# A fused decoder layer: second halves of the up weights at another SBUF place, key scores by query block, no zero matmuls

## The reference, cut to what matters

```python
def peer(x, w_query, sub_keys_1, sub_keys_2, expert_down, expert_up):
    q = (x @ w_query).reshape(B, S, PEER_HEADS, 2, PEER_QDIM // 2)
    s1 = jnp.einsum('bshc,kc->bshk', q[..., 0, :], sub_keys_1)
    s2 = jnp.einsum('bshc,kc->bshk', q[..., 1, :], sub_keys_2)
    ...
    # top 16 of each half -> 256 candidates -> top 16, softmax: gates and expert_idx
    u = expert_down[et]
    h = jax.nn.gelu(jnp.einsum('cd,ced->ce', xt, u), approximate=False)
    vv = expert_up[et]
    return jnp.einsum('ce,ced->cd', gt * h, vv)
```

## Time and profile before

| | |
|---|---|
| median of 3 runs | 2463.01 us (2461.73 to 2466.8) |
| the profiled execution | 2464.3 us |
| its span, first to last instruction | 2462.6 us |
| mean granted TensorE clock | 0.997 |
| TensorE matmuls busy | 2432.2 us, 99% of the span |
| VectorE, ScalarE, GpSimd busy | 60%, 47%, 23% |
| chain that ended last | PE 98% (L1119 66%, L1324 28%) |

### The profile page before, as it was taken

The page is one execution under the profiler, slowest core; times in us unless marked ns, Lnnn a source line. Parts: engine busy times, 40 slices in busy tenths (PEclk is TensorE's granted clock), DMA queues, the critical chain, the costliest instruction groups (busy, mean ns, idle before and its releaser), DMA issues.

```text
span 2462.6 us, 49767 instructions
## 1 busy us (share of the span) xinstructions
PE 2432.2 (99%) x17939; PEld 2292.9 (93%) x17940; DVE 1487.3 (60%) x2444; ACT 1166.8 (47%) x1660; POOL 556.0 (23%) x379
## 2 busy tenths in 40 slices
PE   8999999999999999999999999999999999999997
PEld 8999999999999999999999999999888888888886
DVE  5555554546666667688888644444555555555556
ACT  5444444554544445655555544444444444444444
POOL 0000000000000000468888888800000000000000
PEclk9999999999999999999999999999999999999999
DMA  7767766554445655578888888876766777667764
GB/s 266 223 216 229 225 215 197 190 186 153 153 154 171 196 194 177 170 214 214 208 226 214 218 218 213 222 254 214 234 231 234 240 243 239 226 238 241 241 231 140
DMA packets 179845, 521.15 MB, mean 212 GB/s; under 512 B 52768, under 2 KB 52768, under 8 KB 179536
## 3 DMA queue, kind: packets, MB, share of 16 engines
q1 hardware_dynamic: 124128, 449.89, 56.0%
q0 software_dynamic: 51056, 53.83, 10.1%
q10 hardware_dynamic: 4608, 16.78, 1.7%
HBM read 484.64 MB, written 35.78 MB: 211 GB/s over the span
## 4 chain that ended last, share of the span: by engine, by line
PE 98%; DVE 1%; issue 0%; ACT 0%; DMA 0%; ACTq 0%; DVEq 0%; SPq 0%
PE ps L1119 66%; PE ps L1324 28%; PE ps L1158 1%; PE ps L1173 1%; PE ps L1166 0%; PE ps L1160 0%; PE ps L1293 0%; PE ps L1174 0%; PE ps L1153 0%; DVE u_s L1072 0%; DMA raw<-stream 0%; DVE u_s L1082 0%; DVE y_s L1059 0%; DVE w_first L670 0%; ACTq L603 0%
## 5 line engine op out<-in xcount | busy, mean ns | idle before, releaser
L670 DVE TENSOR_TENSOR w_first<-raw,w_first 128x1024 fp32r<-128x1024 f32 x425 | 520.7, 1225 | 568.0 <-ACT w_first L382 548.5
L1119 PE MATMUL ps<-a_hi,w_first 128*128 128x256 f32 x3728 | 684.2, 279 | 12.3 <-DVE w_first L670 12.3
L1119 PE MATMUL ps<-a_hi,w_second 128*128 128x256 f32 x3728 | 672.6, 276 | 0.0
L670 DVE TENSOR_TENSOR w_second<-raw,w_second 128x1024 fp32r<-128x1024 f32 x425 | 520.0, 1223 | 165.3 <-ACT w_second L382 165.2
L1119 PEld LDWEIGHTS ps<-a_hi,w_first 128*128 128x128 f32 x3728 | 581.0, 188 | 13.2 <-issue 9.1
L1119 PEld LDWEIGHTS ps<-a_hi,w_second 128*128 128x128 f32 x3728 | 578.6, 188 | 0.0
L382 ACT ACTIVATE w_second<-raw 128x1024 fp32r<-128x1024 f32 x425 | 448.0, 1054 | 186.9 <-PE ps L1324 183.7
L1119 PE MATMUL ps<-a_lo,w_first 128*128 128x256 f32 x1864 | 516.3, 277 | 0.0
L1119 PE MATMUL ps<-a_lo,w_second 128*128 128x256 f32 x1864 | 514.6, 276 | 0.0
L353 POOL DMA_INDIRECT g_dram<-gate_v,where x256 | 459.4, 1795 | 114.7 <-issue 80.4
L382 ACT ACTIVATE w_first<-raw 128x1024 fp32r<-128x1024 f32 x425 | 447.8, 1054 | 30.9 <-issue 14.1
(11 more groups left out here) (205 smaller groups left out, 2483.6 us busy)
## 6 DMA issues: line engine op xcount, KB each, us to landing
raw<-stream SPq DMA_DIRECT2D x850, 512.0 KB
g_dram<-blank POOLq DMA_DIRECT2D x32, 512.0 KB, 6.2
a_dram<-act ACTq DMA_DIRECT2D x32, 512.0 KB
a_in<-a_dram POOLq DMA_DIRECT2D x32, 512.0 KB, 5.1
g_in<-g_dram POOLq DMA_DIRECT2D x32, 512.0 KB, 6.3
g_dram<-gate_v,where POOLq DMA_INDIRECT x256
res<-x_t SPq DMA_DIRECT2D x4, 512.0 KB, 6.7
ln_s<-ln POOLq DMA_DIRECT2D x1, 2048.0 KB, 7.5
```

Of the source, the lines that this page charges most:

```text
L670: dve.tensor_tensor(w_lo[s][:, :], raw[:, s, :], w_hi[s][:, :].bitcast(F32), ALU.subtract).then_inc(lo_ready, 1)
L1119: ins = pe.matmul(out, w, a, start=first and q == 0, stop=last and q == 2)
```

## The change

The second halves of the up weights, from up tile 2 on, are split into `up_hi` and `up_lo`. These are views into `a_hi` and `a_lo`, 16 elements (64 bytes) behind their start, at 128 modulo 512. The tiles 0 and 1 keep `w_second`, since their halves are split while the down stage still reads `a_hi` and `a_lo`. The first round of 8 up tiles is written out ahead of the loop on ScalarE, VectorE and TensorE. The zero matmuls, `zero`, and VectorE's memset with its wait are gone; the first up tile starts its banks with `start=True`. Score groups and transposes alternate the token block (`g % 2`) and go through the query blocks in order (`g // 2`); each waits for the blocks that it reads. A wait for `h1_lo` stands ahead of the down loop.

```diff
-    zero = sb("zero", [P, 512], mybir.dt.bfloat16, up_mem)
+    up_hi = a_hi.rearrange("p k t -> p (k t)")[:, 16:16 + 2 * HALF].rearrange("p (s n) -> p s n", s=2)
+    up_lo = a_lo.rearrange("p k t -> p (k t)")[:, 16:16 + 2 * HALF].rearrange("p (s n) -> p s n", s=2)
+
+    def weights(t, hf, moved=False):
+
+        return (up_hi[:, t.par, :], up_lo[:, t.par, :]) if moved and hf else (w_hi[t.slot(hf)], w_lo[t.slot(hf)])
...
-                act.activation(w_hi[t.slot(hf)][:, :], raw[:, t.slot(hf), :], ACT.Copy).then_inc(hi_ready, 1)
+                act.activation(weights(t, hf, moved)[0], raw[:, t.slot(hf), :], ACT.Copy).then_inc(hi_ready, 1)
...
-            act.activation(sc[:, g // 4, 4 * (g % 4):4 * (g % 4) + 4, :], spare[g % 4].rearrange("p (a n) -> p a n", a=4),
+            act.activation(sc[:, g % 2, 4 * (g // 2):4 * (g // 2) + 4, :], spare[g % 4].rearrange("p (a n) -> p a n", a=4),
...
-            act.activation(h1_n[:, g // 4, 512 * (g % 4):512 * (g % 4) + 512], spare[g % 4], ACT.Copy).then_inc(ht_ready, 1)
+            act.activation(h1_n[:, g % 2, 512 * (g // 2):512 * (g // 2) + 512], spare[g % 4], ACT.Copy).then_inc(ht_ready, 1)
...
-                hi(t.next())
+                hi(t.next(), moved=not first or b > 0)
...
-        with act.Fori(0, NKEYS // 8 - 1) as i:
+        up_tiles(0, False, True)
+        with act.Fori(1, NKEYS // 8 - 1) as i:
...
-                dve.tensor_tensor(w_lo[s][:, :], raw[:, s, :], w_hi[s][:, :].bitcast(F32), ALU.subtract).then_inc(lo_ready, 1)
+                high, low = weights(t, hf, moved)
+                dve.tensor_tensor(low, raw[:, s, :], high.bitcast(F32), ALU.subtract).then_inc(lo_ready, 1)
...
-        dve.wait_ge(ag_in[0], 32)
-        dve.memset(zero[:], 0.0).then_inc(z_ready, 1)
...
-        pe.wait_ge(q_done, KD)
         pe.wait_ge(keys_in, 16)
         for g in range(8):
-            tt, c0 = g // 4, 4 * (g % 4)
+            tt, c0 = g % 2, 4 * (g // 2)
+            pe.wait_ge(q_done, c0 + 4)
...
         for g in range(8):
-            tt, c0 = g // 4, 4 * (g % 4)
+            tt, c0 = g % 2, 4 * (g // 2)
             pe.wait_ge(sc_ready, g + 5) if g < 4 else pe.wait_ge(ht_ready, g - 3)
-            pe.wait_ge(h1_ready, KD)
+            pe.wait_ge(h1_ready, c0 + 4)
...
+        pe.wait_ge(h1_lo, KD)
...
-        pe.wait_ge(z_ready, 1)
...
-        for c in range(8):
-            pe.matmul(ps[:, 512 * c:512 * c + 512], zero[:, 0:P], zero[:], start=True, stop=False, skip_group_check=True)
-
-        def up(t, n, b):
+
+        def up(t, n, b, moved=True, first=False):
...
+                high, low = weights(t, hf, moved)
                 for tt in range(TT):
                     s = slice(P * tt, P * tt + P)
-                    for m, w in ((m_hi, w_hi), (m_hi, w_lo), (m_lo, w_hi)):
+                    for q, (m, w) in enumerate(((m_hi, high), (m_hi, low), (m_lo, high))):
                         for c in range(2):
                             o = D * tt + HALF * hf + 512 * c
-                            ins = pe.matmul(ps[:, o:o + 512], m[:, b % 2, s], w[t.slot(hf)][:, 512 * c:512 * c + 512],
-                                            start=False, stop=False, skip_group_check=True)
+                            ins = pe.matmul(ps[:, o:o + 512], m[:, b % 2, s], w[:, 512 * c:512 * c + 512],
+                                            start=first and q == 0, stop=False, skip_group_check=True)
...
-        with pe.Fori(0, NKEYS // 8 - 1) as i:
+        for b in range(8):
+            up(Tile(T_UP + b), b, b, b > 1, b == 0)
+        with pe.Fori(1, NKEYS // 8 - 1) as i:
```

More of the change, by code:

```diff
@@ L252, in build @@
     m_ready, mhi_ready, mlo_ready, y_ready = sem("m_ready"), sem("mhi_ready"), sem("mlo_ready"), sem("y_ready")
-    z_ready, nmean_ready, sd_ready, out_ready, y_done = (
-        sem("z_ready"), sem("nmean_ready"), sem("sd_ready"), sem("out_ready"), sem("y_done"))
+    nmean_ready, sd_ready, out_ready, y_done = (
+        sem("nmean_ready"), sem("sd_ready"), sem("out_ready"), sem("y_done"))
     dve_step, act_step = sem("dve_step"), sem("act_step")
+    up_hi = a_hi.rearrange("p k t -> p (k t)")[:, 16:16 + 2 * HALF].rearrange("p (s n) -> p s n", s=2)
+    up_lo = a_lo.rearrange("p k t -> p (k t)")[:, 16:16 + 2 * HALF].rearrange("p (s n) -> p s n", s=2)
+    def weights(t, hf, moved=False):
+        return (up_hi[:, t.par, :], up_lo[:, t.par, :]) if moved and hf else (w_hi[t.slot(hf)], w_lo[t.slot(hf)])
     r_sq = h1_n.rearrange("p t (q n) -> p (t q) n", q=2)
@@ L375, in _, with hi @@
             act.sem_inc(a_out[b], 16)
-        def hi(t, halves=(0, 1)):
+        def hi(t, halves=(0, 1), moved=False):
             for hf in halves:
@@ L628, in _, with up_tiles @@
             gelu(t, b, NKEYS // 8 - 1)
-        def up_tiles(i, last):
+        def up_tiles(i, last, first=False):
             for b in range(8):
@@ L663, in _, with lo @@
         dve.sem_inc(m_ready, 8)
-        def lo(t, halves=(0, 1)):
+        def lo(t, halves=(0, 1), moved=False):
             for hf in halves:
@@ L1041, in up_tiles @@
                     break
-                lo(t.next())
+                lo(t.next(), moved=not first or b > 0)
                 n = i * 8 + b if not last else NKEYS - 8 + b
@@ L1048, in up_tiles @@
                 m_low(n + 1, (b + 1) % 2)
-        with dve.Fori(0, NKEYS // 8 - 1) as i:
+        up_tiles(0, False, True)
+        with dve.Fori(1, NKEYS // 8 - 1) as i:
             up_tiles(i, False)
@@ L1332, in up_bank @@
             w = slice(512 * (c % 2), 512 * (c % 2) + 512)
[L1333 to L1336, removed]
-        with pe.Fori(0, NKEYS // 8 - 1) as i:
+            high, low = weights(t, c // 2, True)
+            pe.matmul(ps[:, o:o + 512], m_hi[:, b % 2, s], high[:, w], start=False, stop=False, skip_group_check=True)
+            pe.matmul(ps[:, o:o + 512], m_hi[:, b % 2, s], low[:, w], start=False, stop=False, skip_group_check=True)
+            return pe.matmul(ps[:, o:o + 512], m_lo[:, b % 2, s], high[:, w], start=False, stop=False, skip_group_check=True)
+        for b in range(8):
+            up(Tile(T_UP + b), b, b, b > 1, b == 0)
+        with pe.Fori(1, NKEYS // 8 - 1) as i:
             for b in range(8):
```

## The result

The changed kernel takes **2451.14 us** (2450.02 to 2451.9, 6 runs), and the one before 2463.2 us (2461.73 to 2466.8, 6 runs) beside it: ratio 0.9946, with a 95% interval of 0.9935 to 0.9956. That is 0.54% less. The prediction said 2451.9 us. The profiled execution takes 2450.02 us, and its span is 2448.3 us.

A forecast was written before the change was run, and what follows sets the result against it. TensorE's own stream was taken to bound the kernel: 4.2 + 1.4 + 5.5 = 11.1 us off the profiled 2464.3 gives 2453.2, and with the runs' median 1.3 us lower, 2451.9 us; 8-in-10 range 2449.5 to 2457.8.

The forecast's parts named there:

- Key scores: At the scores behind the query projection: waiting by group removes TensorE's idle time and the low clock, 4.2 us less.
- All three parts: At the key scores: 2.45 us of idle time, 1.65 us of low clock and 0.1 us in the first group.
- the scores don't gain: Rival at the key scores: first copy late or clock falls anyway, the wait only moves; 2456.1 us, 8% chance.
- Zero matmuls: Between down and up stage: without the zeros the first up matmul starts earlier, 1.4 us less, ends 1.3 and 1.5.
- hand-over: At the first up rows: 0.2 us of the starts put down to the change from the zeros, some of it remaining.
- Moved halves: In the up stage: second halves at 128 modulo 512 save 0.044 us a tile over 126 tiles, 5.5 us less.
- The settled pace: In the up stage: 229 against 233 ns per matmul, giving the moved halves' upper end of 6.0 us.
- the place modulo 512: In the up stage: the moving operand's place, 128 against 256, makes matmuls take 229 instead of 233 ns.
- The rule that spoke against it: Skill's "PE and ACT never wait on anyone": by it the up stage's moved halves bring 0, the sum 5.6 us.
- A slower rhythm: Rival in the up stage: new halves settle 8 ns slower per matmul, 24.2 us more, 2476.1 us; 6% chance.

The follow-up runs named there:

- experiment 8: Kernel before with `w_second` itself at 128 modulo 512 in every stage, no new home: 2466.64 us, from 2458.42 to 2488.84 in 12 runs, ratio 1.0022.
- Experiment 3: Changed kernel with the moved halves 48 instead of 16 elements into `a_hi` and `a_lo`, at 256 modulo 512: 2457.46 us, ratio 0.997.
- experiment 4: Changed kernel with the second halves at eight places 64 bytes apart, by the tile's position in a round: 2454.91 us in one run.
- experiment 5: Changed kernel with 64 bytes ahead of `m_f`, taking `m_hi` and `m_lo` to 128 modulo 512, halves unmoved: 2445.16 us, ratio 0.9922.
- Experiments 7: Changed kernel with the old order of score groups, each still waiting only for its own columns: five times from 2450.06 to 2456.39 us, ratio 0.9961.

## Why the prediction held

**What bounds the kernel.** TensorE's stream alone did. The marks of its stream add up to the whole difference of the spans, and no other engine came newly late: the waits of TensorE that are left were there before, the one on the gelu at another matmul.

**Key scores, 4.2 us; measured 4.33, and 4.34 alone.** All three parts came: no idle time, the clock at 1.00, groups every 0.89 us. The gap between the starts closed from 2.72 to 0.12 us, which gives 2.60 where 2.45 was taken, and the scores themselves take 7.14 us where they took 8.88, which gives 1.74 where 1.65 + 0.1 was. ScalarE was in time for the fifth group as worked out: its four copies take 0.51 us each, the first ends at about 1023.0, and the group starts at 1020.05 + 4 x 0.89 = 1023.6. The rival *the scores don't gain* falls. That the order of the groups is needed for this was implied, and no profile shows it.

**Zero matmuls, 1.4 us; measured 1.69.** The term was under-sized and lies outside its own ends of 1.3 and 1.5. The 1.32 us between the two rows of rows 7 are not what the zeros cost: the profile of before has rows of only seven of the eight, and the first up row starts too soon behind them. The profile of experiment 8 has all eight:

```profile
1757.69 1.89 PE L1312 MATMUL ps<-zero 128*128 128x512 bf16 x8 [0.56 <-ACT act L599]
```

The first starts 0.84 us behind the last down matmul (1756.85), near the 0.79 at which the first up matmul starts now. Eight of 215 to 216 ns are 1.72 us, and that is what came, less 0.03. No hand-over has to be called in. Tile 1 had 0.55 us to spare, against 0.5 worked out.

**Moved halves, 5.5 us; measured 5.87.** The term was under-sized by 0.4 us: it took 0.044 us a tile. The settled pace gave 6.0, the end that the prediction kept for the range, and that is the one nearer to the measurement. The twelve distances on a first half sum to 2750.8 ns before and 2746.7 after, since the first halves lost their slow entry too; on a second half, 2789.2 before and 2746.7 after. That is 46.6 ns a tile, or 5.87 us in 126 tiles; 5.80 of it lie ahead of the last wait, and the last two tiles have the rest.

**The reason given for it was half right.** Experiment 3 shows that the place did it. But "the place modulo 512" is wrong twice: the period is 256 bytes (experiment 4), and the distance to the stationary operand counts (experiment 5), in which 128 is only the better of the two places that this kernel happened to have. The time came out all the same, because `m_hi` and `m_lo` stayed where they were, so that place and distance changed together; as to the reason, that was luck.

Nor is the distance all of it. `c_hi` and `b_hi` lie at the same place, go with the same weight buffers, and so have the same distance, and show two paces. `b_hi` alone shows both, in one execution: 276 ns from 850 to 925 us, and before that

```profile
L1119 PE MATMUL ps<-b_hi,w_second x192: 278/279/280, 579.7 to 734.4; 128*128 128x256 f32 x192
```

With experiment 8 this shows that the matmuls of 256 columns can take one of two rhythms at the same addresses. What chooses it was not found.

**The rule that spoke against it.** The Trainium skill, SBUF — State Buffer, under "Who interferes with whom", has it that TensorE waits for nobody. The sentence is about other engines, and no run here speaks against that. The step from it to a gain of 0 is what fails: experiments 3 and 5 give 226.7 to 233.3 ns for the same matmul, by the addresses of its own two operands.

**A slower rhythm.** It didn't come in the up stage. It exists: most of the down stage of experiment 8 has it, 117.8 against 113.3 ns, and the loss outdoes the up stage's gain by far. The rival had named the right mechanism and the wrong place.

**The sum.** 11.1 us were predicted, 11.8 are in the changed places, and 12.1 between the medians. All three terms were a little too small, by 0.1, 0.3 and 0.4 us.

## What to carry over

Where TensorE never waits and two groups of equal matmuls still differ by a few ns, compare where their moving and stationary operands lie modulo 256 bytes; padding of 64 bytes took another 6 us off the changed kernel. Move a buffer only for the stage that gains, and look at the pace of every other stage that uses it, in more than one execution: with `w_second` moved for all stages, the same program ran in anything from 2458 to 2489 us. And split a wait for "all columns" by what each group reads: besides the idle time it saved 1.7 us of low clock.

## What was not expected

**Paces by distance.** In the up stage, where each matmul of 512 columns has a weight load of its own, the distance of starts was 226.7 ns at distance 0 modulo 256 and up to 233.5 elsewhere, mostly in patterns of two, three or four matmuls that repeat (226, 229, 232 at distance 64; 231, 236 at 192), but an even 230 at 48. What in the chip makes them was not found. The Trainium skill, TensorE: Matmul & The Clock Gate, under "Back-to-back issue gap", gives about 131 ns for each matmul of 512 columns in a stream with weight loads; no stretch of the up stage comes under 226.7 in these runs. The zeros, in bfloat16 with one stationary operand, stand 215 to 216 ns apart.

**A DMA that takes 3 us to issue.** The untouched down stage was 1.43 us shorter in the profile after. TensorE waits there at two places for VectorE's split; the distances between starts were 1.91 and 1.86 us before, and 1.43 and 1.11 after. The first wait comes behind ScalarE's first store of activations, whose issue is long on its queue, while all later ones are short. In the changed kernel:

```profile
1053.50 3.13 ACTq L609 DMA_DIRECT2D a_dram<-act  x1
1076.41 0.34 ACTq L609 DMA_DIRECT2D a_dram<-act  x1
```

Before, the first takes longer still:

```profile
1058.84 3.61 ACTq L603 DMA_DIRECT2D a_dram<-act  x1
```

The first distance follows this issue: in all twelve profiles it is the issue's time less 1.70 us, from 2.41 and 0.71 in experiment 5 to the 3.61 and 1.91 of before. Over the eleven profiles behind the prediction (the changed kernel and ten runs) the first distance ran from 0.71 to 1.87 us and the second from 0.88 to 1.96, with no relation to what was changed. They account for a profile being a microsecond or two off its kernel's median. The same goes for the stages ahead of the query projection's end, which are the same code except in experiment 8, and took 0.2 to 1.1 us less than in the profile of before in all ten others. So the 2.4 us that the two profiles differ by beyond the changed places are scatter and no gain.

**Two levels with the same addresses.** Experiments 7 and 8 have executions 5.5 and some 20 us apart with nothing changed. For experiment 8 one long execution is seen, and the down stage's rhythm behind its second wait makes the difference; for experiment 7 nothing is known of the long ones.
